# Splitting the end of the first mixer by token block in a two-layer decoder kernel on one Trainium2 core

## What is computed

```python
def even_mixer(x, w_in, ...):            # layer 0
    p = x @ w_in
    y_a = rwkv7_mix(p[..., :RWKV_COLS], ...)     # 8 heads x 64, a recurrence over tokens
    y_b = mlstm_mix(p[..., RWKV_COLS:], ...)     # 4 heads x 128: q, k, v, o, gates
    return jnp.concatenate([y_a, y_b], -1) @ w_out

def mlstm_mix(p, ...):
    q, k, v, o, ig, fg = split_cols(...)
    ...
    h = head_norm(h, hn_g, hn_b, LN_EPS)
    return jax.nn.sigmoid(o) * h

def rwkv7_mix(p, ...):
    ...
    y = head_norm(y, ln_g, ln_b, RWKV_GN_EPS)
    y = y + jnp.sum(r_h * k_h * r_k, -1, keepdims=True) * v_h
    return y * g

def peer_ffn(x, w_q, sub_k1, sub_k2, u_tab, v_tab):   # for each block of 128 tokens
    q = x @ w_q                                        # 8 heads x 2 halves x 128
    s1, s2 = q[:, :, 0] @ sub_k1.T, q[:, :, 1] @ sub_k2.T
    # top 16 of each half, top 16 of the 256 sums -> eid, gate: 8 x 16 experts a token
    act = gelu(sum(x * u_tab[eid]))
    return sum(gate * act * v_tab[eid])

x = layer_norm(DN_ALPHA * x + mixer(x), ln1_g, ln1_b)
x = layer_norm(DN_ALPHA * x + peer_ffn(x), ln2_g, ln2_b)
```

## Time and profile before

| | before |
|---|---|
| median of 3 runs | 1804.92 us |
| profiled execution | 1806.65 us |
| its span | 1804.5 us |
| PE busy | 1544.5 us (86%) |
| DVE busy | 1063.3 us (59%) |
| ACT busy | 604.9 us (34%) |
| POOL busy | 579.8 us (32%) |
| moved | 638.32 MB, 354 GB/s over the span |
| chain of waits that ended last | PE 49%, DMA 37%, DVE 6%, ACT 5% |

### The profile page before, as it was taken

How to read it: one execution, slowest core, us unless ns; L and a number is a source line. 1 busy time by engine, 2 the same in 40 slices (tenths; PEclk the granted TensorE clock), 3 DMA queues, 4 the chain that set the end, 5 groups by cost and what they waited for, 6 DMA issues and landing times.

```text
span 1804.5 us, 18617 instructions
## 1 busy us (share of the span) xinstructions
PE 1544.5 (86%) x6020; PEld 925.0 (51%) x6020; DVE 1063.3 (59%) x2499; ACT 604.9 (34%) x1759; POOL 579.8 (32%) x561
## 2 busy tenths in 40 slices
PE   8999998898777778998899978998999968777776
PEld 7779887754222225763456525763457523222222
DVE  1583543577888865334555447665555568864444
ACT  1434311233333333227532323336632333332222
POOL 2000000334443442333433432334432434444331
PEclk9999858999999999999999999998999999999999
DMA  6222003899999999999999999999999999999996
GB/s 246 95 92 72 1 11 130 342 390 419 419 420 419 420 420 413 419 419 420 419 415 419 414 420 416 420 419 420 419 378 419 405 420 421 419 420 420 420 419 260
DMA packets 92063, 638.32 MB, mean 354 GB/s; under 512 B 11072, under 2 KB 13120, under 8 KB 15424
## 3 DMA queue, kind: packets, MB, share of 16 engines
q0 software_dynamic: 73728, 536.90, 72.0%
q1 hardware_dynamic: 18240, 100.24, 14.3%
HBM read 636.05 MB, written 1.05 MB: 353 GB/s over the span
## 4 chain that ended last, share of the span: by engine, by line
PE 49%; DMA 37%; DVE 6%; ACT 5%; issue 2%; POOL 1%; ACTq 0%; SPq 0%; POOLq 0%; DVEq 0%
DMA arena<-l_peer_uv,arena 34%; PE psum L906 21%; PE psum L588 14%; PE psum L887 4%; DVE arena L1716 3%; DMA wring<-l_w_in 2%; PE psum L765 1%; DMA wring<-l_peer_wq 1%; PE psum L681 1%; PE psum L810 1%; PE psum L671 1%; PE psum L680 1%; ACT L1203 1%; POOL arena L555 1%; ACT early L1216 1%
## 5 line engine op out<-in xcount | busy, mean ns | idle before, releaser
L555 POOL DMA_INDIRECT arena<-l_peer_uv,arena x512 | 566.7, 1107 | 1112.0 <-PE psum L906 851.4
L1716 DVE CUSTOM_DVE_ANT_0 arena<-arena,xres 128x1024 f32<-128x1024 f32 x512 | 620.1, 1223 | 437.8 <-DMA arena<-l_peer_uv,arena 436.4
L906 PE MATMUL psum<-arena,early 128*128 128x512 f32 x1024 | 477.8, 611 | 105.8 <-ACT early L1216 105.8
L906 PE MATMUL psum<-arena 128*128 128x512 f32 x1024 | 476.4, 610 | 106.9 <-ACT arena L1216 106.8
L906 PEld LDWEIGHTS psum<-arena 128*128 128x128 f32 x1024 | 189.8, 193 | 367.9 <-issue 205.6
L906 PEld LDWEIGHTS psum<-arena,early 128*128 128x128 f32 x1024 | 189.4, 193 | 365.4 <-issue 194.6
L588 PE MATMUL psum<-xT,wring 128*128 128x128 f32 (+2 forms) x1856 | 296.5, 320 | 13.6 <-DMA wring<-l_w_in 8.4
L588 PEld LDWEIGHTS psum<-xT,wring 128*128 128x128 f32 (+1 forms) x1856 | 269.2, 192 | 52.5 <-issue 21.0
L1203 ACT ACTIVATE arena<-arena 128x2 f32<-128x2 f32 x256 | 52.1, 203 | 628.4 <-DVE arena L1716 628.2
L1031 ACT COPY arena<-psum 128x256 f32<-128x256 f32 (+2 forms) x138 | 62.5, 471 | 222.6 <-PE psum L588 125.8
L1208 ACT ACTIVATE arena<-arena 128x1 f32<-128x1 f32 x512 | 123.3, 287 | 23.8
(11 more groups left out here) (236 smaller groups left out, 1149.5 us busy)
## 6 DMA issues: line engine op xcount, KB each, us to landing
wring<-l_w_in SPq DMA_DIRECT2D x47, 1024.0 KB, 9.4
wring<-l_peer_wq SPq DMA_DIRECT2D x24, 1024.0 KB, 9.3
wring<-l_w_out SPq DMA_DIRECT2D x12, 1024.0 KB, 11.3
arena<-l_peer_uv,arena POOLq DMA_INDIRECT x512, 17.8
ln_par<-l_ln_g SPq DMA_DIRECT2D x6, 512.0 KB, 12.4
ln_par<-l_ln_b SPq DMA_DIRECT2D x6, 512.0 KB, 15.6
arena<-l_peer_keys SPq DMA_DIRECT2D x2, 1024.0 KB, 7.0
xT<-x_t SPq DMA_DIRECT2D x1, 1024.0 KB, 5.0
```

Source lines behind the costliest of these rows:

```text
L555: pool.indirect_dma_start(out=ring[:, g % RING, :], out_offset=None, in_=T[f"l{l}_peer_uv"], in_offset=bass.IndirectOffsetOnAxis(ap=eid[:, ...
L906: last = mm(self.ps[c], diag[k % DIAGS], ring[:, g % RING, D + c * 512:D + (c + 1) * 512], start=not self.begun, stop=True, skip_group_che ...
L1716: v.tensor_tensor_reduce(out=u, in0=u, in1=xres[:, self.b, :], scale=1.0, scalar=0.0, op0=ALU.mult, op1=ALU.add, accum_out=hid[:, self.b, ...
```

## The change

The four strips of values and output gate no longer stand ahead of the inversion. The values' two strips are projected in chunk 0 of the recurrence and the output gate's two in chunk 1, one between `seq_x` and `seq_u` and one between `seq_u` and `seq_s`; the values are projected with the tokens in the rows, so their transposes (`mv_turn`) go. The head norms, the transposes, the mixing, the out projection, the residual's norm and the first query are each done by token block. Block 0 is projected out behind chunk 2 and ahead of chunk 3; its queries for head 0 and their scores stand ahead of block 1's mixing, and on DVE the routing of head 0 does too. `project_out` now takes all four strips of `l0_w_out` for each block, so they are loaded twice, and the first strip of `l0_peer_wq` is loaded twice as well. The ring's ten places are taken in another order (`RING_PLACES`), since six of them are free in the arena early; the seventh row waits until block 1's out projection has filled its last bank. The buffers behind the ring move (keys, queries, scores). A pair of rows is added on PE and ACT behind block 1's first scores, and DVE does two pairs of dots ahead of the routing of the next heads. From there on the orders are as before.

```diff
-RING = 10
+RING_PLACES = (0, 2, 3, 4, 8, 9, 1, 5, 6, 7)
+RING, EARLY_ROWS = len(RING_PLACES), 6
...
-            ("conv_in", 8), ("bonus", 2), ("token_turn", 6), ("scores", 16), ("ab", 4), ("gates_in", 1), ("vo_in", 4)]
+            ("conv_in", 8), ("bonus", 2), ("token_turn", 6), ("scores", 16), ("ab", 4), ("gates_in", 1)]
...
-    plan += [("mrow_turn", 1), ("mv_turn", 2), ("mx_row", 2), ("qk", 4)]
...
+    plan += [("mrow_turn", 1), ("mx_row", 2), ("qk", 4)]
+    plan += [("seq_x", 1), ("v_in", 1), ("seq_u", 1), ("v_in", 1), ("seq_s", 1), ("seq_y", 1), ("hnum", 2)]
+    plan += [("seq_x", 1), ("o_in", 1), ("seq_u", 1), ("o_in", 1), ("seq_s", 1), ("seq_y", 1), ("h_turn", 1), ("hnum", 2)]
+    plan += [("seq_x", 1), ("seq_u", 1), ("seq_s", 1), ("seq_y", 1), ("y_turn", 1), ("mix_out", 2)]
+    plan += [("seq_x", 1), ("seq_u", 1), ("seq_y", 1), ("h_turn", 1)]
+    plan += [("x_turn", 2), ("peer_q", 1), ("peer_s", 1), ("y_turn", 1), ("mix_out", 2)]
+    plan += [("x_turn", 2), ("peer_q", 2), ("peer_s", 1), ("experts", 2)]
...
-        add_strips("l0_w_in", M0 + 2 * MW, M0 + 4 * MW, "vo_in", 0, 1)
-        add_strips("l0_w_out", 0, D, "mix_out", 0, 1)
+        add_strips("l0_w_in", M0 + 2 * MW, M0 + 3 * MW, "v_in", 0, 1)
+        add_strips("l0_w_in", M0 + 3 * MW, M0 + 4 * MW, "o_in", 0, 1)
+        add_strips("l0_w_out", 0, D, "mix_out", 0, 0.5)
+        add_strips("l0_peer_wq", 0, STRIP, "peer_q", 0, 1)
+        add_strips("l0_w_out", 0, D, "mix_out", 2, 0.5)
...
-            load_strips(16 + WRING - 3)
-            await_filled(sp, "seq_y", NCH - 1)
+            load_strips(16 + 2 - 3)
+            await_filled(sp, "seq_y", 1)
             load_keys(0)
-            load_strips(6 - WRING)
+            load_strips(2 + 1 + 4 + 2)
...
+                    if g == EARLY_ROWS:
+                        await_filled(pool, "mix_out", 3)
...
-                for t in range(4):
-                    w = next_strip(pe)
-                    ps = claim(pe, "vo_in", t)
-                    for q in range(2):
-                        last = project(ps[:, q * SEQ:(q + 1) * SEQ], w, P * q, P)
-                    done(last, "vo_in")
...
+                def value_strip(t):
+
+                    w = next_strip(pe)
+                    ps = claim(pe, "v_in", t)
+                    for b in range(NB):
+                        for k in range(KT):
+                            last = mm(ps[:, b * STRIP:(b + 1) * STRIP], xT[:, k, b * P:(b + 1) * P], w[:, k, :],
+                                      start=(k == 0), stop=(k == KT - 1))
+                    done(last, "v_in")
...
+                pe.wait_ge(S("inv_d_taken"), 4 * len(LEVELS))
+                for c in range(NB):
+                    strip = (value_strip, gate_strip)[c]
+                    chunk_x(c)
+                    strip(0)
+                    chunk_u(c)
+                    strip(1)
+                    chunk_state(c)
+                    chunk_y(c)
+                    if c == 1:
+                        turn_heads("h_turn", h_tok, 0, "h_normed")
+                    if c == 0:
+                        pe.wait_ge(S("v_in_taken"), 2)
+                    values(c)
+                chunk_x(2)
+                chunk_u(2)
+                chunk_state(2)
+                chunk_y(2)
+                turn_heads("y_turn", y_tok, 0, "y_normed")
+                project_out(0)
+                chunk_x(3)
+                chunk_u(3)
+                chunk_state(3)
+                chunk_y(3)
+                turn_heads("h_turn", h_tok, 1, "h_normed")
+                turn_normed(0)
+                pe.wait_ge(S("x_turn_taken"), 2)
+                queries(0, next_strip(pe), slice(0, P))
+                pe.wait_ge(S("keys_loaded"), 16)
+                pe.wait_ge(S("peer_q_taken"), 1)
+                scores(0, 0, [0])
+                turn_heads("y_turn", y_tok, 1, "y_normed")
+                project_out(1)
+                turn_normed(1)
+
+            def project_out(b):
+                pe.wait_ge(S("mixed"), b + 1)
+                for i in range(2):
+                    token_strips("mix_out", 2 * b + i, lambda kt: yT[:, kt, b * P:(b + 1) * P], lambda j: None)
+
+            def turn_normed(b):
+                pe.wait_ge(S("x_normed"), 1 + b)
+                turn_x(2 * b, b)
...
                 pe.wait_ge(S("x_turn_taken"), 4)
-                queries(1, w, slice(P, SEQ))
+                queries(1, next_strip(pe), slice(P, SEQ))
                 queries(2, next_strip(pe), slice(0, SEQ))
                 pe.wait_ge(S("peer_q_taken"), 2)
                 scores(1, 0, [1])
+                ex.pairs(2)
                 for h in range(1, EH):
                     if h < EH - 1:
                         queries(h + 2, next_strip(pe), slice(0, SEQ))
                     pe.wait_ge(S("peer_q_taken"), h + 2)
                     scores(h + 1, h, range(NB))
-                    if h >= HEADS_FIRST - 1:
-                        ex.pairs(2 if h <= HEADS_FIRST else 4)
+                    if h >= 2:
+                        ex.pairs(2 if h <= 3 else 4)
...
+                for c in range(NB):
+                    take = (take_values, take_gate)[c]
+                    take_seq_x(c)
+                    take(0)
+                    take_seq_u(c)
+                    take(1)
+                h_root(1, 0)
+                turned("h_turn", 0)
+                take_seq_x(2)
+                take_seq_u(2)
+                y_root(2, 0)
+                turned("y_turn", 0)
+                take_seq_x(3)
+                take_seq_u(3)
+                h_root(3, 1)
+                turned("h_turn", 1)
                 ln_root(0)
+                take_x(0, 0)
+                y_root(4, 1)
+                queries(0, 0, slice(0, P))
+                scores(0, 0, [0])
+                turned("y_turn", 1)
+                gate_exp(0, *FIRST_GROUPS[0])
                 ln_root(1)
+                take_x(2, 1)
...
+                def finish_block(b):
+                    for i in range(2):
+                        x = xres[:, b, i * 512:(i + 1) * 512]
+                        if (b, i) == (0, 0):
+                            dve.wait_ge(S("x_loaded"), 16)
+                        taken(stt(x, x, ALPHA, full(dve, "mix_out", 2 * b + i), ALU.mult, ALU.add), "mix_out")
+                        dve.wait_ge(S("mix_out_taken"), 2 * b + i + 1)
+                        half_stats(b, i)
+                    layer_norm(b, 2)
+
+                chunk_state(0)
+                chunk_y(0)
+                mlstm_values(0)
+                h_norm(1, 0)
+                chunk_state(1)
+                chunk_y(1)
+                y_norm(2, 0)
+                mlstm_values(1)
+                chunk_state(2)
+                gate_heads(0)
+                chunk_y(2)
+                mix_heads(0)
+                h_norm(3, 1)
+                finish_block(0)
+                chunk_y(3)
+                y_norm(4, 1)
+                gate_heads(1)
+                route(0, 0, FIRST_GROUPS[:1], lambda g, i: None)
+                mix_heads(1)
+                finish_block(1)
...
+            ex.pairs(2)
+            route(0, 0, FIRST_GROUPS[1:], meanwhile)
```

More of the change, by code:

```diff
@@ L747, in mixer0, with chunk_state @@
                     done(last, "seq_u")
+                def chunk_state(c):
+                    b, rows = c // 2, slice(CH * (c % 2), CH * (c % 2) + CH)
                     pe.wait_ge(S("seq_u_taken"), c + 1)
@@ L1121, in mixer0 @@
                             copy(DT[CH:P, us, CH:P], DC[CH:P, 1, us, :]).then_inc(S("d_copied"), 1)
-                for b in range(NB):
-                    taken(copy(vaug[:, b, :, 0:MN], full(act, "mv_turn", b).rearrange("p (h n) -> p h n", h=MH)), "mv_turn")
                 for h in range(MH):
@@ L1134, in turned, with take_values @@
                                   bias=par(bias, t), scale=par(g, t))
-                    taken(last, "y_turn")
-                for c in range(NCH):
+                    taken(last, name)
+                def take_values(t):
+                    ps = full(act, "v_in", t)
+                    for b in range(NB):
+                        last = copy(vaug[:, b, 2 * t:2 * t + 2, 0:MN],
+                                    ps[:, b * STRIP:(b + 1) * STRIP].rearrange("p (h n) -> p h n", n=MN))
+                    taken(last, "v_in")
@@ L1168, in peer_scores0, with scores @@
+            def scores(k, h, blocks):
+                ps = full(act, "peer_s", k).rearrange("p (b q n) -> p b q n", b=NB, q=2)
+                for i, b in enumerate(blocks):
+                    last = copy(sc[b][:, 2 * h:2 * h + 2, :], ps[:, i])
+                taken(last, "peer_s")
+            def peer_scores0(ex):
                 queries(1, 0, slice(P, SEQ))
                 queries(2, 1, slice(0, SEQ))
-                scores(1, 0, 1, 2)
+                scores(1, 0, [1])
+                ex.pairs(2)
@@ L1173, in head, with meanwhile @@
```

(10 more changed lines are left out.)

271 lines of the change are left out of this document (98 added, 173 removed).

## The result

| | before | after |
|---|---|---|
| median of 5 runs | 1805.84 us | 1877.21 us |
| range | 1804.08 to 1809.6 | 1867.44 to 1878.38 |
| profiled execution, its span | 1806.65, 1804.5 us | 1867.44, 1865.7 us |
| PE busy | 1544.5 us | 1572.4 us |
| moved | 638.32 MB | 643.57 MB |

The change makes the kernel slower: ratio 1.0391, 95% interval 1.0368 to 1.0413. The prediction, 1825 us in a range of 1807 to 1842, has the sign, and misses the size by 52 us. The profiled execution of after is the fastest of its five by 8 us; what the other four lost there was not profiled.

The account below looks back on a forecast made before the run. From about 325 us the DMA stream of gathered expert rows, 2.5 us each, was taken as the bound. The stream's lag of 21.9 us, taken as 20, on the median of 1804.92 gave 1825 us, range 1807 to 1842.

Parts of the forecast that it names:

- (a): Ahead of the inversion: strips leaving gain 14.2 us, value transposes 1.0, a half-clock start costs 2.7; recurrence starts at 197.8.
- (b): Recurrence: with the strips inside chunks 0 and 1, chunks 0, 1 and 2 take 21, 25 and 15 us.
- (c): First block: out projection takes 18.2 us, block normed at 292.9, 10.7 us earlier than before; first gather at 313.7.
- (d): Second block: TensorE waits some 12 us behind head 0's routing, projection takes 20.6; its queries begin 29 us later.
- (e): Heads' queries: the next strip's query starts at 364.5 us, where it was 325.35.
- (f): Gather stream: the ring's ten rows are spent before the queries, so the stream lags 21.9 us, never taken back.
- (g): Out projection and query strip loaded twice: 12.5 us of DMA, costed at nothing extra as it lies in idle DMA time.
- the 2.7 us for a start at half clock: At each of four TensorE starts after idle, the inversion's among them: 2.7 us lost, bounds 0 and 2.7.
- rival 2: Recurrence, chunk 2: full clock there, 13.21 us busy become 6.6, so 1818 us; chance 0.20.
- Rival 4: Inversion: stays at half clock after the new idle, up to 45 us more, 1870 us; chance 0.05.
- the 7.4 that I took as the middle: Second block's out projection: fourth strip lands 7.4 us after its request, between bounds 4.9 alone and 9.7 beside a full stream.
- rival 1: Gather stream: early rows pay, as the stream counts from its first gather, 20.0 us earlier; about 1797 us; chance 0.08.

Follow-up runs that it names:

- with 10 and 22: The changed kernel plus 10 and 22 extra 128x256 matmuls in TensorE's two waits ahead of the inversion: 1833.32 us.
- a_w22_noearly: The changed kernel with 10 and 22 extra matmuls, and no gather issued before block 1's out projection has filled its last bank: 1827.86 us.

## Why the prediction was wrong

| step | predicted | after | with 10 and 22 |
|---|---|---|---|
| (a) recurrence starts | 197.8 | 237.02 | 196.72 |
| (b) chunks 0, 1, 2 | 21, 25, 15 | 20.4, 24.1, 11.8 | |
| (c) out projection of block 0 | 18.2 | 17.6 | 17.2 |
| first gather, from the start | 115.9 | 111.4 | 112.3 |
| (d) wait before block 1's projection | 12 | 11.46 | 11.46 |
| (d) that projection | 20.6 | 24.5 | 26.5 |
| (e) next strip's query, from the start | 166.7 | 164.5 | 171.0 |
| (f) lag of the end | 21.9 | 61.2 | 27.2 |

**Step (a) failed**, in one term: the 2.7 us for a start at half clock, with bounds of 0 and 2.7. Without the term the recurrence was forecast at 195.1; it started at 237.02, so the term measured 41.9 us, and 44.1 when counted from the gates' strip, which began 2.2 us earlier in after. The 2.7 came from 32 records of 128x128 after an idle time of 4.56 us, behind which the clock came back; I took the price of such a start for a property of the start. The runs show that it is one of the work that follows: the inversion's 128x64 matmuls keep a full clock and don't regain a lost one, so that a wait of 2.56 us costs half of the speed of all of the inversion behind it.

The trace of before could have said it. In the recurrence TensorE was busy for 49.09 of 54 us at 0.50, and I used that very row against rival 2 for chunk 2, where 6.6 us hung on it, and not for the inversion, where 45 did. Rival 4 had the mechanism and the time (up to 1870), and I gave it 0.05, "it held full with the same matmuls": true, and no answer, since holding and regaining are two things. Step (a) itself has TensorE "without work from 131 to 142"; the wait was seen, and its price was not bounded from the far side.

**Steps (b) to (e) held** in after: block 1 was normed at +142.1 for +143.1. Two terms were off. Chunk 2 kept its clock until about 287 (0.73 in the window), so it took 11.8 for 15: rival 2 was half right, and it changed the sign of nothing. The fourth strip landed 9.5 us after its issue (359.78 to 369.32), at the upper bound of 9.7 and not in the 7.4 that I took as the middle. With the clock repaired, this landing, 9.97 us, and a pair of rows at half clock (6.54 us for 3.67) explain the most of 27.2 against 21.9; some 2 us stay open.

**(f) held in its mechanism**, and less exactly in its size than 22.0 beside 21.9 suggests. In after the query stands 2.2 us early, counted from the recurrence's start (164.5 for 166.7), and behind it 2.3 us more are lost than foretold, so two errors cancel. Between the medians the lag is 71.4 us: 43.9 of them are the clock (1877.21 to 1833.32 with 10 and 22), and the other 27.5 stand against the 20 that the forecast had. Early rows buy nothing, as the ring's ten rows wait for TensorE anyway, and rival 1 falls with `a_w22_noearly`.

**(g) stays open.** The bytes loaded twice were not tried alone; with the value strips ahead and block 1 mixed first, the split with all its extra bytes stands 5 us above the kernel before, between the medians.

The Trainium skill (TensorE: Matmul & The Clock Gate, What's actually happening) says that the clock depends on how busy the engine has been recently. If busy means what the profile calls busy, this case disagrees: 88.92 us of 88.92 at 0.50. Which work counts, the records can't say; between the two kinds here, 128x256 regained the clock in each place shown here where it was lost, and 128x64 in none.

## What to carry to other kernels

Before moving dense work away from ahead of a long stretch of narrow matmuls, ask what TensorE does right before the first of them: here a wait of 2.6 us cost some 45 us, and three spare matmuls more in it, on top of 26 that had not been enough, gave them back. Price a fall of the clock by the length of the narrow work behind it, not by the wait, and use dense work that is needed anyway (a projection strip) as the filler. When a second block waits on the routing of the first, look for the small step (two products of 0.69 us) that can go ahead of it.

## What the runs showed that was not expected

- The same 128x64 matmuls ran a level of the inversion in 10.7 us (163.15 to 173.87 before) or in 20.5 (153.39 to 173.87 after), at a busy share of one in both. The first two lines are the starts of two levels before, the last two in after:

```profile
163.15 3.74 PE L671 MATMUL psum<-arena 128*128 128x64 f32 x32
173.87 3.74 PE L671 MATMUL psum<-arena 128*128 128x64 f32 x32
...
153.39 7.04 PE L664 MATMUL psum<-arena 128*128 128x64 f32 x32
173.87 7.04 PE L664 MATMUL psum<-arena 128*128 128x64 f32 x32
```

- Waits of 6.59, 6.34, 2.57 and 2.56 us right ahead of them went with 0.50 for the whole inversion; 1.27, 0.37, 0.32 and none with 1.00.
- An experiment that adds filler can fail for a few matmuls: 26 of them left the time at 1877, 29 brought it to 1832.
- Code that is the same in both kernels doesn't start at the same time: the gates' strip began at 115.05 in after and between 114.58 and 119.78 in runs with the same work ahead of it. A difference of under 5 us between two profiles should be counted from a point behind that.
